# Filler matmuls on TensorE at the end of the norms, in the rank norm and in the log gates of a four-block transformer program

## The chip, the cores and the metric

The kernel runs on one core of a Trainium2 chip (trn2) as one program. The metric is the device time of one execution in microseconds (us). The median of three runs is 4041.17 us.

## The reference

Two blocks of two layers each, on 512 tokens of width 1024, all in fp32. The code below is cut to the order of the work.

```
# first block, 2 layers: mixer, norm, routed experts, norm
h = layer_norm(alpha*h + swa_sink_gqa(h, ...))      # layer 0: window attention
h = layer_norm(alpha*h + hier_moe(h, ...))          # 32 experts, 2 per token
h = layer_norm(alpha*h + mla(h, ...))               # layer 1: latent attention
      # inside mla: c = x @ w_down; cq = rms_norm(c[:384]); ckv = rms_norm(c[384:640])
h = layer_norm(alpha*h + hier_moe(h, ...))
# second block, 2 layers, on the 512 tokens and 256 context tokens
mod = silu(c) @ w_ada + b_ada                       # shifts, scales, gates
u = modulate(rmsnorm(x, g), sh1, sc1) @ w_in        # norms x0, x1
g_f = log_sigmoid(glr_f @ wg2_fw + bg_fw) / 16      # log gates lg0, lg1 (g_b likewise)
x = x + g1 * (concat(gla, short_conv, neighbourhood_attention) @ w_out)
h = modulate(rmsnorm(x, g), sh2, sc2)               # norms f0, f1
x = x + g2 * conv_ffn(h, ...)
return rmsnorm(x, final_norm_g)
```

The filler matmuls of the change compute nothing of this.

## The kernel before, in words

The program is a row of stages. Each stage is one block in which every engine has its own list of instructions, written out by hand, with semaphores between them; `end()` (L137) closes it with a barrier of all engines, in two steps of which the second follows the clearing of the semaphores. So no engine begins a stage before all have ended the one ahead. Weights are the exception: `issue` lets SyncE load the first four weight tiles of the next stage while the present one still runs.

The large products are run in fp32 split into a high and a low part (fp32r): three matmuls of up to 512 columns in place of one. ScalarE casts a weight tile (`w_high`), VectorE subtracts (`w_low`), TensorE multiplies: high by high, low by high, high by low. `fused_stream` (L694) and `stream` (L456) do this for the projections, `ffn_up` (L3331) for the feed-forward part. At the start of each of these stages TensorE waits until the first tile has gone through ScalarE and VectorE.

The change touches four places in the lists of TensorE:

- `norm` (L1061 to L1144) normalises rows on VectorE and ScalarE. TensorE has no instruction in it. It is called twice: for the two low-rank parts of the latent attention ("b_norms", the rank norm), with `issue`, and for the last norm, without. Behind the rank norm come two short stages (the rotary turn, L1155 to L1160, and a copy, L2367), and then the up projection.
- `norm_turn` (L1163 to L1371) normalises token tiles and turns them. Statistics are taken tile by tile on VectorE (L1231 to L1236), ScalarE takes the root (L1318) and normalises (L1297, L1299), TensorE transposes the tile in eight pieces of 128x128 into the eight PSUM banks (L1351), and VectorE and ScalarE empty the banks by turns with scale and shift (`evac`, L1193 and L1195). With context tokens there are two parts, tiles 0 to 3 and 4 to 5; the second part's transposes wait, bank by bank, for the first part's evacuation. Where the next stage is `fused_stream` or `ffn_up` (`"XS" in turn`), the turned rows are split here too: ScalarE casts (L1304), VectorE subtracts (L1259). With `"logits"` TensorE goes on to the router's product.
- `norm_turn` is called for the norm ahead of the latent attention (m0_ln: four tiles, with XS, and with the weighted sum of the experts' rows; VectorE ends it with L1253 and L1254), by `modulated` for the mixing norms x0 and x1 (six tiles, two parts, no XS) and the feed-forward norms f0 (six tiles, two parts, XS) and f1 (four tiles, XS). The calls with logits and the one without `turn` are left as they are.
- `log_gates` (L2732 to L2809) has TensorE transpose the low-rank columns (L2771) and multiply them by the gate weights (L2778, 12 fp32 matmuls per layer, 17 rows deep, into banks 0 to 5); VectorE and ScalarE then take log sigmoid in three rounds (L2789, L2791, L2805, L2808, L2794). The next stage is neighbourhood attention (L927, masked and reduced on VectorE at L979, with the bias tables at L2714).

The matmul at L3089, in the gated linear attention, is plain fp32 with 512 columns.

```
if "logits" in turn:
    w = turn["logits"][1]
for t in range(NTT):
    pe.wait_ge(low_v, 1 if t < NT else 2)
    pe.wait_ge(low_a, 1 if t < NT else 2)
```

These two pieces, of `norm_turn` and of `log_gates`, are the surroundings of the lines added.

Of the kernel before, what the change touches and what calls it, by code (L numbers as in the profile page):

```python
# [23 lines left out]
BANK = 512  # L24
# [96 lines left out]
class Program:  # L121
# [29 lines left out]
    def load(self, name, pairs):  # L151

        nc, sem = self.nc, self.Sems(self, name)
        loaded_sp, loaded_act = sem("loaded_sp"), sem("loaded_act")
        with nc.Block() as block:
            @block.sync
            def _(sp):
                for dst, src in pairs[0::2]:
                    sp.dma_start(dst, src).then_inc(loaded_sp, 16)
                sp.wait_ge(loaded_sp, 16 * len(pairs[0::2]))  # L160

            @block.scalar
            def _(act):
                for dst, src in pairs[1::2]:
                    act.dma_start(dst, src).then_inc(loaded_act, 16)
                if len(pairs) > 1:
                    act.wait_ge(loaded_act, 16 * len(pairs[1::2]))
        self.end(sem)

    def transpose(self, name, groups, beside=None, loads=None):  # L170

# [889 lines left out]
    def norm(self, name, tiles, kind, eps, loads=(), issue=None):  # L1061

        nc, sem = self.nc, self.Sems(self, name)
        stats, roots, scales, step, loaded = (sem(n) for n in ("stats", "roots", "scales", "step", "loaded"))
        normed, gained, biased = sem("normed"), sem("gained"), sem("biased")
        ctx = ExitStack()
        n = len(tiles)
        pieces = [[(c, min(c + 512, t[0].shape[1])) for c in range(0, t[0].shape[1], 512)] for t in tiles]  # L1070
        bn = self.sbuf(ctx, "bn", [P, n, 12])
        mv = self.sbuf(ctx, "mv", [P, n, 4])
        inv = self.sbuf(ctx, "inv", [P, n, 2])
        eps_t = self.sbuf(ctx, "eps", [P, 1])
        gains, biases = tiles[0][2] is not None, tiles[0][3] is not None
        by_act = [gains or i % 2 == 1 for i in range(n)]
        with nc.Block() as block:  # L1077
            if loads:
                @block.sync
                def _(sp):  # L1080
                    for dst, src in loads:
                        sp.dma_start(dst, src).then_inc(loaded, 16)
                    if issue:
                        issue(sp)

            @block.vector
            def _(dve):
                order = Order(dve, step)
                order.done(dve.memset(eps_t[:, :], eps))  # L1089
                for i, (src, dst, gain, bias) in enumerate(tiles):  # L1090
                    for c, (a, b) in enumerate(pieces[i]):
                        ins_ = dve.bn_stats(bn[:, i, 6 * c:6 * c + 6], src[:, a:b])  # L1092
                    order.done(ins_)
                for i in range(n):
                    ins_ = dve.bn_aggr(mv[:, i, 0:2], bn[:, i, 0:6 * len(pieces[i])])  # L1095
                order.done(ins_)
                if kind == "rms":
                    order.done(dve.tensor_tensor(mv[:, :, 2], mv[:, :, 0], mv[:, :, 0], ALU.mult))  # L1098
                    order.done(dve.tensor_tensor(mv[:, :, 2], mv[:, :, 2], mv[:, :, 1], ALU.add))  # L1099
                else:  # L1100
                    order.done(dve.tensor_copy(mv[:, :, 2], mv[:, :, 1]))
                dve.sem_inc(stats, 1)  # L1102
                dve.wait_ge(roots, 1)
                order.done(dve.reciprocal(inv[:, :, 0], mv[:, :, 3]))  # L1104
                if kind == "ln":
                    order.done(dve.scalar_tensor_tensor(out=inv[:, :, 1], in0=mv[:, :, 0], scalar=-1.0,
                                                        in1=inv[:, :, 0], op0=ALU.mult, op1=ALU.mult))
                dve.sem_inc(scales, 1)  # L1108
                if loads:
                    dve.wait_ge(loaded, 16 * len(loads))  # L1110
                for i, (src, dst, gain, bias) in enumerate(tiles):
                    if not by_act[i]:
                        dve.tensor_scalar(dst, src, inv[:, i, 0:1], None, ALU.mult)
                    if gains:
                        dve.wait_ge(normed, i + 1)  # L1115
                        dve.tensor_tensor(dst, dst, gain, ALU.mult).then_inc(gained, 1)  # L1116
                if biases:
                    dve.wait_ge(gained, n)
                    dve.tensor_tensor(dst, dst, bias, ALU.add)

            @block.scalar
            def _(act):
                act.wait_ge(stats, 1)
                act.activation(mv[:, :, 3], mv[:, :, 2], ACT.Sqrt, bias=eps_t[:, :]).then_inc(roots, 1)  # L1124
                act.wait_ge(scales, 1)
                for i, (src, dst, gain, bias) in enumerate(tiles):
                    if not by_act[i]:
                        continue
                    if kind == "rms":
                        act.activation(dst, src, ACT.Copy, scale=inv[:, i, 0:1]).then_inc(normed, 1)  # L1130
                    else:
                        act.activation(dst, src, ACT.Identity, bias=inv[:, i, 1:2],
                                       scale=inv[:, i, 0:1]).then_inc(normed, 1)

            @block.gpsimd
            def _(pool):
                if biases:
                    pool.wait_ge(loaded, 16 * len(loads))
                    for i, (src, dst, gain, bias) in enumerate(tiles[:-1]):
                        pool.wait_ge(gained, i + 1)  # L1140
                        pool.tensor_tensor(dst, dst, bias, ALU.add).then_inc(biased, 1)
                    pool.wait_ge(biased, n - 1)
        ctx.close()
        self.end(sem)  # L1144
# [18 lines left out]
    def norm_turn(self, name, tiles, kind, eps, loads=(), combine=None, finish=None, turn=None, beside=None, issue=None):  # L1163
# [19 lines left out]
        items = [(k, part) for part in range(len(turn["parts"])) for k in range(KD)] if turn else []  # L1183
# [18 lines left out]
        with nc.Block() as block:  # L1202
# [137 lines left out]
            if turn:  # L1340
                @block.tensor
                def _(pe):
                    for t in range(n):
                        part = [i for i, (a, b, _, _) in enumerate(turn["parts"]) if a <= t < b][0]
                        first = turn["parts"][part][0]
                        pe.wait_ge(normed, t + 1)
                        for k in range(KD):
                            if part and t == first:
                                i = items.index((k, part - 1))
                                pe.wait_ge(out_v if by_dve[i] else out_a, count[i])  # L1350
                            ins_ = pe.transpose(self.ps[:, k, (t - first) * P:(t - first + 1) * P],  # L1351
                                                tiles[t][1][:, k * P:(k + 1) * P], self.const("ident"))
                        ins_.then_inc(turned, 1)
                    if "logits" in turn:
                        w = turn["logits"][1]
                        m = w.shape[2]
                        pe.wait_ge(loaded, 16 * len(loads))
                        for k in range(KD):
                            pe.wait_ge(out_v if by_dve[k] else out_a, count[k])
                            for t in range(n):  # L1360
                                ins_ = pe.matmul(self.ps[:, 0, t * m:(t + 1) * m], turn["XT"][:, k, t * P:(t + 1) * P],
                                                 w[:, k, :], start=(k + t == 0), stop=(k == KD - 1),
                                                 skip_group_check=True)
                        ins_.then_inc(summed, 1)
# [1367 lines left out]
    def log_gates(self, layer, UG, LR, MX, beside, loads):  # L2732
# [8 lines left out]
        with ExitStack() as ctx:  # L2741
# [6 lines left out]
            ident = self.const("ident")  # L2748
# [7 lines left out]
            with nc.Block() as block:  # L2756
# [11 lines left out]
                def _(pe):  # L2768
# [5 lines left out]
# [3 lines that stand above are left out]
                        for d in range(2):  # L2777
                            ins_ = pe.matmul(Z(t)[:, d * QK:(d + 1) * QK], LR[:, d, t * P:(t + 1) * P],  # L2778
                                             W2[:, d * QK:(d + 1) * QK], start=True, stop=True)
                        ins_.then_inc(products, 1)  # L2780

                @block.vector
                def _(dve):
# [730 lines left out]
```

## Time and profile before

| | |
|---|---|
| runs | 4038.2, 4041.17, 4041.52 us |
| profiled execution | span 4027.6 us from the first to the last instruction, 51130 instructions; no other time of it is given. The median of the runs is 13.6 us above the span |
| TensorE (PE) busy | 3484.0 us, 87% of the span |
| VectorE (DVE) busy | 2580.3 us, 64% |
| ScalarE (ACT) busy | 2238.7 us, 56% |
| GpSimd (POOL) busy | 588.4 us, 15% |
| DMA | 643.21 MB, mean 160 GB/s |

The eight places of the change lie in the span like this (from barrier to barrier): m0_ln 818 to 858 us, rank norm 893 to 904, x0 1878 to 1899, log gates lg0 2138 to 2156, f0 2484 to 2513, x1 3090 to 3110, log gates lg1 3314 to 3332, f1 3596 to 3616.

In the profile PE is TensorE's matmuls. "PEclk" is the granted TensorE clock of a stretch as a share of full speed, and its two levels are 0.50 (1.2 GHz) and 1.00 (2.4 GHz). The row of a group of instructions gives its start, its length, the engine, the line, and in brackets how long the engine had been idle before it and what ended that.

### The profile page before, as it was taken

How to read it: one execution, taken by the hardware profiler on the slowest of the kernel's cores; microseconds unless marked ns; L12 is line 12 of the kernel's file. 1: busy time of each engine (PE TensorE's matmuls, PEld its weight loads, DVE VectorE, ACT ScalarE, POOL GpSimd, SP SyncE). 2: the span in 40 equal slices, each digit the busy share in tenths (PEclk: the TensorE clock that was granted, in tenths of full speed). 3: DMA queues.
4: the chain of work that ended last, by engine and by line, in shares of the span. 5: the costliest groups of instructions: out<-in, count | busy, mean ns of one | idle time of the engine just before them, and what ended most of it. 6: DMA issues, size and time to landing. Idle time of an engine off the chain costs nothing. (4 is left out here: it accounts for less than half of the span.)

```text
span 4027.6 us, 51130 instructions
## 1 busy us (share of the span) xinstructions
PE 3484.0 (87%) x17582; PEld 2850.1 (71%) x17582; DVE 2580.3 (64%) x3499; ACT 2238.7 (56%) x2862; POOL 588.4 (15%) x284
## 2 busy tenths in 40 slices
PE   8869999848969999857987887999997988869997
PEld 7757777647757777635887765888776877558875
DVE  4669999845569999886455555444445565645545
ACT  3549999834449999775344553333233444634433
POOL 0005333400005334400002220000000002300000
PEclk9879999979979999978998968999999998879999
DMA  3049999921049999894110000211121220012222
GB/s 108 30 155 415 418 419 415 366 97 45 26 174 419 417 417 414 343 377 198 57 50 32 2 32 33 73 62 62 55 63 45 72 64 5 1 61 102 94 86 81
DMA packets 139776, 643.21 MB, mean 160 GB/s; under 512 B 22110, under 2 KB 35808, under 8 KB 76000
## 3 DMA queue, kind: packets, MB, share of 16 engines
q1 hardware_dynamic: 129260, 623.44, 40.2%
q0 software_dynamic: 10080, 16.80, 1.1%
q8 instruction: 86, 1.41, 0.1%
q10 hardware_dynamic: 288, 1.05, 0.1%
q14 instruction: 62, 0.51, 0.0%
HBM read 636.77 MB, written 24.36 MB: 164 GB/s over the span
## 5 line engine op out<-in xcount | busy, mean ns | idle before, releaser
L1647 DVE TENSOR_TENSOR w_low<-w_raw,w_high 128x2048 fp32r<-128x2048 f32 x392 | 881.8, 2283 | 61.8 <-ACT w_high L1644 54.2
L1644 ACT CAST w_high<-w_raw 128x2048 fp32r<-128x2048 f32 x392 | 746.3, 1910 | 87.1 <-DMA w_raw<-in_moe_down_dram 39.4
L1954 PE MATMUL banks<-w_high,x_split 128*128 128x512 f32 x1024 | 421.5, 412 | 43.8 <-DVE w_low L1647 36.6
L1954 PE MATMUL banks<-w_low,x_split 128*128 128x512 f32 x1024 | 408.2, 399 | 0.0
L456 PE MATMUL banks<-w_high,x_high 128*128 128x512 f32 (+2 forms) x808 | 309.8, 383 | 53.5 <-DVE w_low L373 29.0
L337 ACT CAST w_high<-w_raw 128x512 fp32r<-128x512 f32 (+2 forms) x200 | 117.8, 589 | 421.7 <-PE banks L456 415.6
L3331 PE MATMUL banks<-x_high,w_high 128*128 128x512 f32 (+1 forms) x1056 | 318.7, 356 | 28.1 <-DVE w_low L3371 28.1
L3331 PE MATMUL banks<-x_low,w_high 128*128 128x512 f32 (+1 forms) x1056 | 318.2, 355 | 0.0
L3331 PE MATMUL banks<-x_high,w_low 128*128 128x512 f32 (+1 forms) x1056 | 317.9, 355 | 0.0
L456 PE MATMUL banks<-w_low,x_high 128*128 128x512 f32 (+2 forms) x808 | 301.9, 374 | 0.0
L456 PE MATMUL banks<-w_high,x_low 128*128 128x512 f32 (+2 forms) x808 | 301.9, 374 | 0.0
L1954 PEld LDWEIGHTS banks<-w_high,x_split 128*128 128x128 f32 x1024 | 194.4, 190 | 122.4 <-DVE w_low L1647 78.0
L1904 POOL DMA_INDIRECT expert_rows<-ys,sidx x34 | 252.4, 7425 | 125.4 <-ACT ys L2124 124.8
L3356 ACT ACTIVATE convolved<-banks,taps 128x768 f32<-128x768 f32 (+1 forms) x88 | 77.9, 885 | 297.1 <-PE banks L3331 297.1
L694 PE MATMUL banks<-w_high,x_high 128*128 128x512 f32 (+2 forms) x516 | 207.9, 403 | 30.6 <-DVE w_low L664 17.5
L371 DVE TENSOR_TENSOR x_low<-mixT,x_high 128x768 fp32r<-128x768 f32 x112 | 107.3, 958 | 187.9 <-ACT x_high L338 187.7
L1954 PEld LDWEIGHTS banks<-w_low,x_split 128*128 128x128 f32 x1024 | 195.0, 190 | 40.6
L456 PEld LDWEIGHTS banks<-w_high,x_high 128*128 128x128 f32 x808 | 155.0, 192 | 96.9 <-DVE w_low L373 43.8
L3331 PEld LDWEIGHTS banks<-x_high,w_high 128*128 128x128 f32 x1056 | 175.0, 189 | 56.9 <-issue 28.7
L3383 DVE SCALAR_TENSOR_TENSOR convolved<-banks,taps,convolved 128x511 f32<-128x511 f32 (+1 forms) x132 | 83.0, 656 | 194.1 <-ACT convolved L3356 194.1
L694 PE MATMUL banks<-w_high,x_low 128*128 128x512 f32 (+2 forms) x516 | 203.3, 394 | 0.0
L694 PE MATMUL banks<-w_low,x_high 128*128 128x512 f32 (+2 forms) x516 | 203.1, 394 | 0.0
(411 smaller groups left out, 7576.8 us busy)
## 6 DMA issues: line engine op xcount, KB each, us to landing
w_raw<-in_moe_gate_dram SPq DMA_DIRECT2D x132, 1024.0 KB, 10.5
w_raw<-in_moe_up_dram SPq DMA_DIRECT2D x132, 1024.0 KB, 10.2
w_raw<-in_moe_down_dram SPq DMA_DIRECT2D x132, 1024.0 KB, 10.9
w_raw<-in_w_ada_dram SPq DMA_DIRECT2D x48, 1024.0 KB, 12.9
w_raw<-in_ffn_w_up_dram SPq DMA_DIRECT2D x44, 1024.0 KB, 4.8
w_raw<-in_ffn_w_down_dram SPq DMA_DIRECT2D x88, 256.0 KB, 2.7
w_raw<-in_w_cols_dram SPq DMA_DIRECT2D x48, 256.0 KB, 2.6
w_raw<-in_w_out_dram SPq DMA_DIRECT2D x32, 256.0 KB, 3.0
```

The source lines that it names most:

```text
L337: act.copy(WS[0][:, rest % S, 0:w], W[:, rest, 0:w])
L371: dve.tensor_tensor(XS[1][:, rest % S, :], x_tile(k), XS[0][:, rest % S, :].bitcast(F32), ALU.subtract)
L456: ins_ = pe.matmul(psum_of(g), st[:, rest % S, a:b], mv[:, rest % S, x:y], start=start and first + second == 0, stop=stop and first == 1)
L694: ins_ = pe.matmul(psum_of(g), XS[first][:, k, t * P:(t + 1) * P], WS[second][:, u % S, 0:w], start=(i == 0 and first + second == 0), stop ...
L1644: act.copy(ex["WS"][0][:, v % HIGH, :], ex["WR"][:, v % RAW, :]).then_inc(ex["high"], 1)
L1647: dve.tensor_tensor(ex["WS"][1][:, v % LOW, :], ex["WR"][:, v % RAW, :], ex["WS"][0][:, v % HIGH, :].bitcast(F32), ALU.subtract).then_inc( ...
L1904: pool.indirect_dma_start(out=Y, out_offset=bass.IndirectOffsetOnAxis(ap=sidx[:, 0:1], axis=0), in_=YS[:, :], in_offset=None, bounds_check ...
L1954: ins_ = pe.matmul(GU[b][m], stationary(b, kk), WS[w][:, s, k * BANK:(k + 1) * BANK], start=(kk == 0 and w == 0), stop=(kk == KD - 1 and w ...
L3331: ins_ = pe.matmul(U(b, ab)[:, x:y], WS[first][:, b, at:at + P], XS[second][:, k, x:y], start=(k == 0 and first + second == 0), stop=(k == ...
L3356: act.activation(Z[:, ab, :], U(b, ab)[:, 0:ntok], ACT.Identity, bias=cv[:, bass.ds(f * 8 + (4 * ab + 3), 1)], scale=cv[:, bass.ds(f * 8 + ...
L3383: dve.scalar_tensor_tensor(out=z[:, x + 1:y], in0=u[:, x:y - 1], scalar=cv[:, bass.ds(f * 8 + 4 * ab, 1)], in1=z[:, x + 1:y], op0=ALU.mult ...
```

## The change

A new helper multiplies the identity (128x128, fp32) by the first 512 columns of the table of constants (fp32) into one whole PSUM bank, `count` times, with no semaphore; nothing reads the bank.

- in `norm` (only where `issue` is given, so in the rank norm): 10 times, into bank 0, without waiting for anything; TensorE had no work in this stage.
- in `norm_turn` without logits: behind all transposes, TensorE waits until bank 0's last part has been emptied, and then multiplies 8 times (with XS: m0_ln, f0, f1) or 3 times (x0, x1) into bank 0.
- in `log_gates`: 8 times into bank 7 right behind the products of both layers. Bank 7 held a group of transposes that ScalarE has emptied before the first product.

These are 10 + 3 x 8 + 2 x 3 + 2 x 8 = 56 matmuls in the source. Nothing is removed or moved.

```diff
+    def keep_busy(self, pe, bank, count):
+
+        for _ in range(count):
+            ins_ = pe.matmul(self.ps[:, bank, :], self.const("ident"), self.consts[:, 0:BANK], start=True, stop=True)
+        return ins_
...
@@ norm, behind the list of ScalarE
+            @block.tensor
+            def _(pe):
+                if issue:
+                    self.keep_busy(pe, 0, 10)
+
...
@@ norm_turn, behind the transposes
                         ins_.then_inc(turned, 1)
+                    if "logits" not in turn:
+                        i = items.index((0, len(turn["parts"]) - 1))
+                        pe.wait_ge(out_v if by_dve[i] else out_a, count[i])
+                        self.keep_busy(pe, 0, 8 if "XS" in turn else 3)
                     if "logits" in turn:
...
@@ log_gates, behind the products
                         ins_.then_inc(products, 1)
+                    self.keep_busy(pe, 7, 8)
```

Line numbers in the texts are those of the kernel before; in the changed kernel the matmul of `keep_busy` is L173.

## Rows read from the trace of the kernel before

**Rows 1.** Spans and mean granted clock of the core.
```profile
core 0: 4027.6 us, clock 0.918
```

**Rows 2.** Windows, TensorE: stretch, length, busy (records), PEclk, DMA share, GB/s.
```profile
859.42:864.66 5.24, 5.24 (x16) 0.50 0.50 150
864.66:869.66 5.00, 5.00 (x30) 1.00 0.21 59
1902.70:1905.72 3.02, 3.02 (x9) 0.50 0.43 128
3113.66:3117.45 3.79, 3.79 (x9) 0.50 0.42 137
2519.08:2523.53 4.45, 4.45 (x14) 0.50 0.66 236
3622.47:3626.04 3.57, 3.57 (x8) 0.50 0.67 223
```

**Rows 3.** Waits of VectorE, 3331 to 3352 us: in total, times, longest.
```profile
DVE scores L979 <- PE banks L927: 0.7, 2, 0.5
```

**Rows 4.** Timeline of L3089, then L3089 and L2778: records, ns min/median/max.
```profile
2272.09 5.38 PE L3089 MATMUL banks<-mixT,k_end 128*64 128x512 f32 x6 [2.67 <-POOL mixT L3037]
3498.26 2.79 PE L3089 MATMUL banks<-mixT,k_end 128*64 128x512 f32 x6
...
L3089 PE MATMUL banks<-mixT,k_end x144: 592/592/1117, 2272.1 to 3506.4; 128*64 128x512 f32 x144
...
L2778 PE MATMUL banks<-w_gate,lowrankT x48: 320/322/523, 2141.5 to 3323.1; 17*128 17x192 f32 x48
```

**Rows 5.** Timeline of VectorE in m0_ln.
```profile
846.93 1.53 DVE L1193 TENSOR_SCALAR qT<-banks,columns 128x512 f32<-128x512 f32 x2
...
856.00 1.22 DVE L1254 TENSOR_TENSOR H<-H,bias 128x1024 f32<-128x1024 f32 x1
```

**Rows 6.** Windows of TensorE around two idle stretches.
```profile
2039.19:2042.06 2.87, 0.00 (x0) 1.00 0.17 62
2042.41:2047.41 5.00, 2.28 (x6) 0.50 0.16 43
3941.54:3947.00 5.46, 2.61 (x11) 1.00 0.20 54
```

**Rows 7.** Timeline: VectorE in the rank norm, TensorE behind it.
```profile
902.75 0.42 DVE L1116 TENSOR_TENSOR o_rows<-o_rows,gkv 128x256 f32<-128x256 f32 x1
...
907.53 1.94 PE L685 MATMUL banks<-consts,o_rows 128*128 128x128 f32 x8 [16.00 <-PEq L139]
```

**Rows 8.** Timeline of VectorE in x0; windows of TensorE behind x0's and x1's transposes.
```profile
1896.86 1.90 DVE L1193 TENSOR_SCALAR mixT<-banks,scale,MC 128x256 f32<-128x256 f32 x4 [3.58 <-PE banks L1351]
...
1896.82:1902.70 5.88, 0.00 (x0) 0.50 0.00 0
3107.63:3110.60 2.97, 0.00 (x0) 1.00 0.00 0
```

**Rows 9.** Timeline of VectorE in f0 and f1.
```profile
2506.15 0.54 DVE L1193 TENSOR_SCALAR hiddenT<-banks,scale,MC 128x256 f32<-128x256 f32 x1 [1.71 <-PE banks L1351]
...
2510.50 1.42 DVE L1259 TENSOR_TENSOR x_low<-hiddenT,x_high 128x256 fp32r<-128x256 f32 x4
...
3612.78 2.55 DVE L1259 TENSOR_TENSOR x_low<-hiddenT,x_high 128x512 fp32r<-128x512 f32 x4
```

**Rows 10.** Windows of TensorE over f1's transposes.
```profile
3601.24:3607.39 6.15, 5.85 (x32) 0.65 0.00 1
```

**Rows 11.** Timeline: VectorE's last in the log gates, TensorE's first in attention.
```profile
2151.89 2.88 DVE L2794 SCALAR_TENSOR_TENSOR mixT<-banks,mixT 128x384 f32<-128x384 f32 x6 [3.06 <-ACT mixT L2808]
...
2155.93 0.76 PE L927 MATMUL banks<-nakT_high,naqT 128*128 128x512 f32 x1 [9.50 <-PEq L139]
...
3327.90 2.88 DVE L2794 SCALAR_TENSOR_TENSOR mixT<-banks,mixT 128x384 f32<-128x384 f32 x6 [3.06 <-ACT mixT L2808]
...
3331.94 0.77 PE L927 MATMUL banks<-nakT_high,naqT 128*128 128x512 f32 x1 [8.29 <-PEq L139]
```

## The prediction

> **What bounds the kernel now.** I read the clock first. TensorE's mean granted clock is 0.918 of full speed over a span of 4027.6 us [rows 1]. The clock has two levels, so it stood at the lower one (1.2 GHz) for 2 x (1 - 0.918) = 16% of the span, some 660 us. The change works on only eight places of it. Then I took the stretch behind each place by windows. Where TensorE has been idle at the end of a norm, the next stage's dense matmuls begin at 0.50: for 5.24 us behind the latent norm m0_ln, 3.02 and 3.79 behind the mixing norms x0 and x1, 4.45 and 3.57 behind the feed-forward norms f0 and f1 [rows 2]. The rank norm's successor I take to be like m0_ln's. Sixteen matmuls took 5.24 us there; 30 took 5.00 us right after, so sixteen would have taken 2.67 and the slow clock cost 2.6 us, 0.49 of the stretch. By that share the six stretches (20.1 us and once more 5.2) cost 12.4 us, 0.3% of the run. That is all that the norms could give back. The log gates come before attention, and there VectorE waited for TensorE's first products for only 0.7 us in the first 20 us [rows 3]: attention starts at VectorE's pace, so a warm clock gives at most that.
>
> **The price of one filler.** keep_busy multiplies plain fp32. The trace has such a matmul of 512 columns at L3089: six records in a row took 5.38 us with the clock low and 2.79 with it high. A record on its own lasts 1.12 us at the most and 0.59 at the least, so the steps are (5.38 - 1.12)/5 = 0.85 and (2.79 - 0.59)/5 = 0.44 us, of which 0.43 is taken. One fp32 matmul of the source is two records: L2778 is called 12 times per layer, 24 in all, and has 48 [rows 4]. So a filler takes **0.86 us at the high clock, 1.71 at the low**. Eight take 6.9, three 2.6, ten 8.6 at the high clock. At the low clock the rise comes after some time of dense work, 4.0 us in the mean of five stretches (5.24, 3.02, 3.79, 4.45, 3.57) [rows 2]: eight then take 4.0 + (8 - 4.0/1.71) x 0.86 = 8.9 us, three take 4.0 + 0.66 x 0.86 = 4.6. The last record ends 0.16 us later than its step.
>
> **What the fillers run beside.** Every stage ends in a barrier of all engines; I take it that TensorE reaches it only when the fillers are done. What counts is whether they end before VectorE's last instruction, and then how long TensorE still idles.
>
> - **m0_ln, 8 fillers.** VectorE empties bank 0 at 846.93 + 0.76 = 847.7 and ends at 857.22 [rows 5]. The clock is low: 847.7 + 8.9 + 0.16 = 856.8. No delay; 0.4 us of cover is left. TensorE then idles until 859.42, 2.7 us. Two idle stretches of that length lie in the trace: after 2.87 us (2039.19) the clock was low, after 2.85 us (3941.54) it stayed at 1.00 [rows 6]. Half of 2.6: **-1.3** (bounds -2.6 and 0).
> - **Rank norm, 10.** TensorE is free 16.00 us before 907.53, at 891.5; a barrier later, near 892.7, the fillers start with the clock high and end at 901.5. VectorE's last ends at 902.75 + 0.42 = 903.17 [rows 7]. No delay. But two short stages follow, and TensorE idles until 907.5, for 6.0 us, twice what lowered the clock at 2039: **0** (bounds -2.6 and 0).
> - **x0 and x1, 3 each.** VectorE empties bank 0's last part first of four in 1.90 us from 1896.86, so the fillers start at 1897.4 with 1.4 us of cover until 1898.76. At the high clock (2.6 + 0.16) they end 1.3 us late, at the low one (4.6 + 0.16) 3.4 late. The same code left the clock low in x0 and high in x1 [rows 8], so I take the mean: 2 x 2.35 = **+4.7** (bounds +2.6 and +6.8). After that, TensorE idles as long as it takes the next stage to cast and subtract its first operands, from 1898.76 to 1902.70 = 3.9 us; that is over 2.9, so nothing comes back.
> - **f0, 8.** From 2506.15 + 0.54 = 2506.7; VectorE ends at 2511.92 [rows 9]. Low clock: 2515.8, 3.8 us late; high clock: 2513.8, 1.8 late. It was low, with transposes coming one by one: **+3.3**. From VectorE's end to the first matmul at 2519.08 are 7.2 us, which stay idle: no gain.
> - **f1, 8.** The transposes end at 3607.39 with the clock high [rows 10]; bank 0 takes 0.77 us, as in m0_ln (two in 1.53) [rows 5]. From 3608.2 to 3615.2; VectorE ends at 3615.33 [rows 9]. **+0.2**, for 0.1 us of cover (+1.9 if low). Then 7.2 us idle, no gain.
> - **Log gates, 8 each.** TensorE is free 9.50 us before 2155.93 and 8.3 before 3331.94, at 2146.4 and 3323.6; clock low. Fillers end at 2155.5 and 3332.7. VectorE ends at 2154.77 and 3330.78 [rows 11]: **+0.7 and +1.9** (clock never rising: +5.6 and +6.8). Only the barrier's one us is idle then, so attention starts warm: 2 x **-0.3**, at most -0.7 each.
>
> The sum is -1.3 + 0 + 4.7 + 3.3 + 0.2 + 0.7 + 1.9 - 0.6 = **+8.9 us**. The profiled span of 4027.6 us has no total of its own; the runs' median of 4041.17 lies 13.6 above it, launch and end, which the change leaves alone. Forecast: 4050.1 us. The terms' own bounds, not all at once, give +4 to +14. What a measurement can tell from no change is 0.2%, 8.1 us, and the forecast lies just over it.
>
> **Transposes and the clock.** From 3601.24 to 3607.39 TensorE did nothing in f1 but transposes by the identity (L1351), 32 of them, and the clock of that stretch is 0.65 in the mean [rows 10]: it came in at 0.50, and for 0.3 of the time, the last 1.8 us, it was at full speed. Transposes lifted the clock here. The Trainium skill (TensorE: Matmul & The Clock Gate, Part 4) says the opposite, that the full clock does not engage for transposes. The trace disagrees. By the page, fillers behind transposes would always start at the low clock, which is the fourth rival below.
>
> **Rivals.**
> 1. *The barrier does not hold the others back* (TensorE passes it with fillers still in flight, so casts of the next stage run under them). Then the delays go, except 0.7 us in lg1 where the matmuls themselves queue; x0 starts warm (fillers end 1902.1, matmuls 1902.70: -1.5), x1 idles some 2.8 us and gains half of 1.9, m0_ln -1.3, attention -0.6. Sum -3.6: 4037.6. It decides wherever fillers outlast VectorE, five places of eight. For it: no row shows a stage that TensorE ended last. Against: every stage begins on all engines at once. Chance 0.10. **This is the case that ends on the other side**, not slower.
> 2. *The clock survives all the idle ends.* Then 12.4 + 0.6 come back against delays of 10.8: -2.2, 4039.0. Against it are rows 6 and the idle of 6 to 7 us. 0.05; with rival 1 as well (-12.4 - 0.6 + 0.7, 4029) 0.02.
> 3. *A filler is one record, not two.* Eight take 5.4 us from low, three 2.6. x0 is 1.4 late, x1 0, f0 0.4, the rest covered; TensorE idles longer after it and nothing comes back: +1.8, 4043. Against it is 48 for 24. 0.06.
> 4. *Fillers always start low* (the page's rule, if f1's rise was luck). x0 and x1 3.4 each, f0 3.8, f1 1.9: the sum becomes +13.2, 4054. 0.07.
> 5. *Constants never lift the clock.* Eight take 13.7 us and 0.27 for the last record: m0_ln +4.4, x0 and x1 +4.0 each, f0 +8.7, f1 +6.8, the gates +5.6 and +6.8: +40, 4081 and more. The rise under L1351, whose one operand is the identity too, speaks against it. 0.03.
>
> **How the numbers follow.** The forecast has 0.67. By its bounds three fifths of it lie above 8.1 us: 0.40, and with rivals 4 and 5, slower is 0.50. Same is 0.27 from it and 0.18 from rivals 1, 2 and 3, 0.45. Faster is rivals 1 and 2 together and the edge of 1: 0.05. The range of 8 in 10 goes from 4039 (rivals 2 and 3 in, 1 out) to 4057 (rival 4 in, 5 out).
>
> **What will show it.** 112 new records of L173 between 0.59 and 1.12 us. The barriers behind x0, x1, f0 and the gates later by 1 to 4 us, behind m0_ln and the rank norm not. The first matmuls behind x0, x1, f0, f1 and the rank norm still at 0.50; attention's at 1.00. I am wrong if ACT's first cast after x0 starts before the last filler ends, if one of the six stretches of rows 2 is warm more than now and then, or if the records are 56.

## The result, and the profile after

The changed kernel takes 4051.11 us in the median of 8 runs (4044.0 to 4061.2), the kernel before 4041.35 us beside it (8 runs, 4031.7 to 4044.5). The ratio is 1.0033, 95% interval 1.0023 to 1.0043: 13.3 us slower, between 9.3 and 17.4. One execution of all in this document (of e7, below) took 11,408 us at a mean granted clock of 0.442; every ratio leaves it out.

The profiled execution of the change took 4049.33 us with a span of 4047.5 us, 19.9 more than the span in [rows 1]. Its core and its clock:

```profile
core 0: 4047.5 us, clock 0.925
```

The granted clock rose (0.918 to 0.925) and the time rose with it. The page has TensorE busy for 62 us more (3484.0 us before):

```profile
PE 3546.0 (88%) x17694; PEld 2867.4 (71%) x17694; DVE 2579.0 (64%) x3499; ACT 2238.5 (55%) x2862; POOL 583.8 (14%) x284
```

The new line of the source, L173: durations in ns (min/median/max), first and last start.

```profile
L173 PE MATMUL banks<-consts x112: 592/592/1223, 847.5 to 3634.5; 128*128 128x512 f32 x112
```

So 56 matmuls are 112 records. The eight stretches of fillers, by windows of TensorE (stretch, length, busy (records), PEclk, DMA share, GB/s), in the order m0_ln, rank norm, x0, x1, f0, f1, lg0, lg1:

```profile
847.46:856.01 8.55, 8.54 (x16) 0.83 0.00 0
891.59:900.43 8.84, 8.82 (x20) 1.00 0.57 158
1894.81:1899.35 4.54, 4.52 (x6) 0.62 0.00 0
3121.73:3127.20 5.47, 5.45 (x6) 0.52 0.00 0
2509.71:2518.29 8.58, 8.56 (x16) 0.83 0.00 0
3627.98:3635.13 7.15, 7.13 (x16) 1.00 0.00 1
2151.38:2159.92 8.54, 8.53 (x17) 0.83 0.01 5
3340.88:3350.30 9.42, 9.41 (x17) 0.76 0.13 51
```

(x17 in the gates: the last gate product lies in the window too.) VectorE's last instruction in m0_ln, x0, x1, f0, f1, lg0 and lg1, by the timeline; these answer to [rows 5, 8, 9, 11]:

```profile
855.65 1.22 DVE L1265 TENSOR_TENSOR H<-H,bias 128x1024 f32<-128x1024 f32 x1
...
1894.22 1.90 DVE L1204 TENSOR_SCALAR mixT<-banks,scale,MC 128x256 f32<-128x256 f32 x4 [3.58 <-PE banks L1362]
...
3121.14 1.90 DVE L1204 TENSOR_SCALAR mixT<-banks,scale,MC 128x256 f32<-128x256 f32 x4 [2.98 <-PE banks L1362]
...
2513.48 1.42 DVE L1270 TENSOR_TENSOR x_low<-hiddenT,x_high 128x256 fp32r<-128x256 f32 x4
...
3632.47 2.55 DVE L1270 TENSOR_TENSOR x_low<-hiddenT,x_high 128x512 fp32r<-128x512 f32 x4
...
2155.80 2.88 DVE L2810 SCALAR_TENSOR_TENSOR mixT<-banks,mixT 128x384 f32<-128x384 f32 x6 [3.07 <-ACT mixT L2824]
...
3346.17 2.88 DVE L2810 SCALAR_TENSOR_TENSOR mixT<-banks,mixT 128x384 f32<-128x384 f32 x6 [3.06 <-ACT mixT L2824]
```

The fillers end 3.2 us behind VectorE in x0 (1899.35 against 1896.12), 4.2 in x1, 3.4 in f0, 1.2 in each of the gates, 0.1 in f1; in m0_ln and the rank norm they end before it. Where they end late, the next stage starts late: after x0 ScalarE's first cast comes 0.9 us behind the last filler.

```profile
1900.25 0.62 ACT L343 CAST w_high<-w_raw 128x512 fp32r<-128x512 f32 x1 [4.10 <-ACTq L337]
```

What came back, by windows over the first matmuls of the next stage; these answer to [rows 2]. In order: behind m0_ln (two windows), x0, x1, f0, f1, and the start of attention behind lg0 and lg1:

```profile
859.07:860.58 1.51, 1.51 (x8) 1.00 0.27 63
860.58:863.99 3.41, 3.41 (x12) 0.50 0.64 203
1903.25:1908.47 5.22, 5.22 (x15) 0.50 0.32 104
3131.24:3137.27 6.03, 6.03 (x14) 0.50 0.27 87
2525.43:2529.70 4.27, 4.27 (x13) 0.50 0.76 242
3642.29:3645.86 3.57, 3.57 (x8) 0.50 0.65 232
2160.83:2166.83 6.00, 3.49 (x16) 1.00 0.01 3
3351.21:3355.73 4.52, 2.59 (x12) 1.00 0.00 0
```

Attention alone starts at the full clock and keeps it over these windows; it falls there too, 7.2 us (lg0) and 4.6 us (lg1) behind the barrier. Behind m0_ln the clock holds for 1.5 us and falls while TensorE is multiplying. Behind x1 the slow stretch is now longer than before, 6.03 us against 3.79 [rows 2]. Behind x0 it is 5.22 us against 3.02 [rows 2], but that is no effect of the fillers: the kernel before has 4.78 and 5.72 us there in two further traces (e9, then e1, below).

```profile
1902.91:1907.69 4.78, 4.78 (x14) 0.50 0.37 110
...
1902.01:1907.73 5.72, 5.72 (x18) 0.50 0.28 92
```

From barrier to barrier, in us, with three more traces that the experiments brought: e1 and e9 are the kernel before, word for word, and e10 is the change, word for word.

| stage | before | e1 | e9 | change | e10 | predicted |
|---|---|---|---|---|---|---|
| m0_ln | 39.95 | 39.96 | 39.91 | 40.00 | 40.26 | 0 |
| behind it (down projection) | 34.48 | 34.35 | 33.98 | 33.66 | 33.64 | -1.3 |
| rank norm | 11.15 | 11.15 | 11.16 | 11.16 | 11.17 | 0 |
| up projection | 58.49 | 58.40 | 58.21 | 55.52 | 58.31 | 0 |
| x0 | 21.22 | 21.18 | 21.22 | 24.40 | 24.48 | +2.35 |
| u0 (projection behind x0) | 238.67 | 240.97 | 240.01 | 242.15 | 242.16 | 0 |
| lg0 | 17.66 | 17.80 | 17.39 | 18.54 | 18.61 | +0.7 |
| attention 0 | 94.71 | 94.69 | 94.82 | 94.20 | 94.80 | -0.3 |
| f0 | 28.36 | 28.35 | 28.36 | 31.72 | 31.87 | +3.3 |
| ffn_up0 (behind f0) | 380.74 | 380.77 | 387.76 | 387.66 | 387.65 | 0 |
| x1 | 20.39 | 20.39 | 20.72 | 24.88 | 24.88 | +2.35 |
| u1 (behind x1) | 203.62 | 203.72 | 203.65 | 204.84 | 205.07 | 0 |
| lg1 | 17.76 | 17.91 | 17.68 | 18.22 | 18.62 | +1.9 |
| attention 1 | 80.58 | 80.42 | 80.38 | 79.52 | 79.50 | -0.3 |
| f1 | 20.10 | 20.09 | 20.10 | 20.22 | 20.17 | +0.2 |
| span | 4027.6 | 4033.9 | 4040.6 | 4047.5 | 4057.7 | |

The puzzle in the first pair of traces was ffn_up0: 6.92 us longer, more than any stage with a filler in it (4.5 at the most), and not at its start but evenly over the whole stage, at the full clock.

### The profile page after: what moved, and what is told of

The parts are those of the page before. It is cut to its first block and busy times, and to the rows that moved or that the text cites. A ratio compares the mean times of both kernels' runs of the same rounds, so it can differ in the third digit from the quotient of the medians.

```text
span 4047.5 us, 51354 instructions
## 1 busy us (share of the span) xinstructions
PE 3546.0 (88%) x17694; PEld 2867.4 (71%) x17694; DVE 2579.0 (64%) x3499; ACT 2238.5 (55%) x2862; POOL 583.8 (14%) x284
```

## The experiments

**e1: the kernel before, word for word**, as a measure of what two traces of one kernel differ by.

> The kernel before, once more, for a second trace of it. The two traces at hand differ by 19.9 us of span but the medians of eight runs by only 9.8. In the first trace the feed-forward up stage of layer 0 took 380.7 us, in the trace of the changed kernel 387.7, at the same granted clock, with matmul steps 1.9% longer from the first to the last. Theory A (the fillers cost what they push the barriers, about 12 us, and the slower pace is chance that a kernel without fillers shows too): the median is within 0.15% of before, and over repeated traces that stage takes now 381, now 388 us. Rival B (the fillers cause the slower pace): it takes 380.7 us here again and whenever there are no fillers.

Measured: 4038.25 us, ratio 1.0006 (0.9996 to 1.0016). Its stages differ from those of before by up to 2.3 us (u0), with nothing changed.

**e2: only the fillers that VectorE's work covers** (m0_ln, rank norm, f1).

```diff
-                    if "logits" not in turn:
+                    if "XS" in turn and len(turn["parts"]) == 1 and "logits" not in turn:
...
-                    self.keep_busy(pe, 7, 8)
```

> Fillers only where they end before VectorE does: m0_ln (8), rank norm (10), f1 (8). Theory A: no barrier moves; the stage behind m0_ln is shorter by 0 to 2.6 us, the one behind the rank norm by 0 to 3, the one behind f1 by nothing: 0 to -5 us in all, 4036 to 4041, the same or a little faster than before. Rival B: as slow as the change as a whole (+8 to +10), since fillers anywhere do it.

Measured: 4036.47 us, ratio 1.0004 (0.9995 to 1.0014). The stages m0_ln, rank norm and f1 took 40.03, 11.15 and 20.25 us, the down projection 33.65. Covered fillers cost nothing and bring 0.6 us (33.65 against the mean of 34.27 in the three traces of the kernel before).

**e3: only the uncovered ones** (x0, x1, f0, log gates).

```diff
-                if issue:
-                    self.keep_busy(pe, 0, 10)
+                pass
...
-                    if "logits" not in turn:
+                    if not ("XS" in turn and len(turn["parts"]) == 1) and "logits" not in turn:
```

> Fillers only where they outlast VectorE: x0 and x1 (3 each), f0 (8), the log gates (8 each). Theory A: all of the loss is here. Barriers later by 1.3 to 4.5 us in x0 and x1 each, 1.8 to 3.9 in f0, 0.4 to 1.9 in each of the log gates; 0.5 to 1 us back in each attention: +7 to +14 us in all, 4048 to 4055, more than the whole change. Rival B: the same loss as with any fillers, +8 to +10.

Measured: 4047.58 us, ratio 1.0035 (1.0019 to 1.0050), the whole loss of the change. x0 22.79, f0 31.94, x1 24.87 us; x0 lost less than in the change because its fillers met the full clock earlier (2.8 us for the three), and in lg0 (17.08 us) the eight ended 0.4 us before VectorE did.

**e4: twice the fillers in x0, x1 (6) and f0 (16)**, the rest as in the change.

```diff
-                        self.keep_busy(pe, 0, 8 if "XS" in turn else 3)
+                        self.keep_busy(pe, 0, 6 if "XS" not in turn else 16 if len(turn["parts"]) > 1 else 8)
```

> The whole change, but twice the fillers in x0, x1 (6 each) and f0 (16). Theory A (the barrier waits for each of them, at 0.86 us once the clock is high): each of x0 and x1 longer by another 2.6 to 3.5 us, f0 by another 6.9, in sum 12 to 14 us more than the change, about 4064. Rival C (the barrier does not wait for TensorE's fillers): the same as the change, 4051.

Measured: 4063.55 us, ratio 1.0062 (1.0046 to 1.0079). f0 took 38.60 us, 6.88 more than in the change for 8 fillers: 0.86 each. x0 took 27.08 and x1 27.44, 2.7 and 2.6 more for three. The log gates, whose eight fillers are those of the change, took 20.46 and 20.41 us in this trace, against 18.54 and 18.22: the clock rose later there, and the fillers ended 2.8 and 2.2 us behind VectorE, where it had been 1.2. The barrier waits for every filler at the price of two records, and the rivals "the barrier doesn't hold the others back" and "one record" fall. The 32 records of f0:

```profile
2518.77:2534.22 15.45, 15.45 (x32) 0.90 0.00 1
```

After these four, ffn_up0 had taken 380.8 (before, e1, e2), 380.6 (e4) and 387.7 us (the change, e3). The numbers of fillers ahead of it are 0, 0, 18, 48 and 37, 19. It looked as if the place of ffn_up0's loop in TensorE's list of instructions, which every filler ahead of it moves ("place" below), or what f0's eight leave behind ("f0"), set the pace.

**e5: one filler in all, in x0. e6: the change with nine in f0.**

```diff
@@ e5
-                    if "logits" not in turn:
+                    if name == "x0":
...
-                        self.keep_busy(pe, 0, 8 if "XS" in turn else 3)
+                        self.keep_busy(pe, 0, 1)
@@ e6
-                        self.keep_busy(pe, 0, 8 if "XS" in turn else 3)
+                        self.keep_busy(pe, 0, 3 if "XS" not in turn else 9 if len(turn["parts"]) > 1 else 8)
```

> One filler in all, in x0 behind its last eviction; nothing else of the change (the rank norm and the layer norm keep an empty TensorE block, which adds one branch ahead of the FFN). The question is why the matmuls of ffn_up0 take 0.1767 us a step instead of 0.1734 in the change and in e3 but not in e2 and e4. Theory 'place': it is where the loop's instructions lie in TensorE's instruction stream, which every filler (4 instructions: two weight loads and two matmuls) and every branch ahead of it moves. Counted so, the loop is moved by 150 in the change and 77 in e3 (slow; 6 and 5 modulo 8), by 74 in e2, 194 in e4 and 0 in before (normal; 2, 2 and 0 modulo 8). Here it is moved by 5: ffn_up0 takes 387.7 us, 7 more than before, and the kernel 4041.35 + 0.9 + 7 - about +8 us, ratio 1.002. Theory 'f0': it is what f0's eight fillers leave behind (the clock's phase, a bank): none here, so ffn_up0 takes 380.7 and the kernel is at 1.0002.

> The change with 9 fillers in f0 instead of 8, all else the same. Theory 'place': ffn_up0's loop is moved by 154 instructions (2 modulo 8, as e2 and e4): ffn_up0 takes 380.7 us, f0 0.86 us more than in the change, and the span is about 6 us under that of the change (4047.5), near 4041.5; ratio 1.0018. Theory 'f0': what eight fillers in f0 leave, nine leave too: ffn_up0 387.7 us, span 4048.4, ratio 1.0035.

Measured: e5 4042.05 us, ratio 1.0004 (0.9994 to 1.0014), ffn_up0 387.75. e6 4050.57 us, ratio 1.0033 (1.0017 to 1.0048), ffn_up0 380.34. Both traces did what "place" said, but both medians did not: e5 without a loss, e6 with the change's whole loss though its trace has the fast pace. So the profiled traces alone can't answer it: a pace that belongs to the kernel would have moved the medians.

**e9, e10, e11: the kernel before, the change and e5 again, word for word.**

> The kernel before, word for word, profiled a third time. The stretch ffn_up0 took 380.74 us in its first trace and 380.77 in e1's; 387.7 in the change, e3, e5, e7 (385.6 with its head at full clock) and e8. Theory 'place' (where the loop lies in TensorE's instructions decides its pace): 380.7 again. Theory 'chance' (the pace is drawn anew in each execution, whatever the kernel: e6's median stands at 1.0033 though its profile has the fast pace, e5's at 1.0004 though its profile has the slow one, and the unchanged kernel alone spans 4031 to 4048 us): 380.7 or 387.7, about as often.

> The change, word for word, profiled again. Theory 'place': ffn_up0 387.7 us as in its first trace. Theory 'chance': 380.7 or 387.7; with 380.7 the span is near 4040.5.

> e5 (one filler in x0) profiled again. Theory 'place': 387.7 us for ffn_up0, as in e5. Theory 'chance': either; over these three runs and e1 'chance' leaves about 1 in 8 that all repeat their first value.

Measured: ffn_up0 took 387.76 us in the unchanged kernel (380.74 and 380.77 in its other traces) and 380.81 in e5's kernel (387.75 in its other). "Place" is refuted. TensorE over the same 250 us of the unchanged kernel, before and then e9:

```profile
2600.00:2850.00 250.00, 250.00 (x1444) 1.00 0.18 66
```

```profile
2600.00:2850.00 250.00, 250.00 (x1417) 1.00 0.18 63
```

And of e5 and then e11, one filler both:

```profile
2600.00:2850.00 250.00, 250.00 (x1417) 1.00 0.18 63
```

```profile
2600.00:2850.00 250.00, 250.00 (x1444) 1.00 0.17 63
```

Same clock, 1.9% fewer matmuls, with nothing changed in the kernel. Of the 14 traces six have the fast pace (before, e1, e2, e4, e6, e11) and eight the slow one. So 7 of the 19.9 us between the first two spans are no effect of the change.

**e8 and e7: can fillers win?** e8 keeps to what fits under VectorE (m0_ln 8, rank norm 11, gates 6, f0 3, f1 8, x0 and x1 none). e7 adds one in the rope behind the rank norm, and fillers past the barrier, at the head of the stage where TensorE waits for its first weights.

```diff
@@ e8 and e7
-                    self.keep_busy(pe, 0, 10)
+                    self.keep_busy(pe, 0, 11)
...
-                    if "logits" not in turn:
+                    if "XS" in turn and "logits" not in turn:
...
-                        self.keep_busy(pe, 0, 8 if "XS" in turn else 3)
+                        self.keep_busy(pe, 0, 3 if len(turn["parts"]) > 1 else 8)
...
-                    self.keep_busy(pe, 7, 8)
+                    self.keep_busy(pe, 7, 6)
@@ e7 alone: rope_halves, stream, ffn_up
+            @block.tensor
+            def _(pe):
+                self.keep_busy(pe, 0, 1)
...
+                if name[0] == "u":
+                    self.keep_busy(pe, 0, 3)
                 tiles(pe, tile)
...
                     pe.sem_inc(multiplied, 4)
+                    self.keep_busy(pe, 0, 6)
```

> As e7 without the fillers in the rope and at the heads of u and of the FFN: 8 in the layer norm, 11 in the rank norm, 6 in the log gates, 3 in f0, 8 in f1. Theory A: no barrier later by more than 0.3 us; gains only b_up -0.4 to -3, na0 -0.5, na1 -1; ratio 0.9990 to 0.9997. ffn_up0 (moved by 114 instructions, 2 modulo 8) at 380.7. What e7 has over this one is the worth of the heads. Rival (a filler at a tail delays the barrier even where VectorE is later): f0 and the log gates +0.5 each, ratio 1.000.

> Fillers only where they can't hold a barrier back, and in the idle heads of the next stages too: 8 in the layer norm, 11 in the rank norm and 1 in the rope that follows, 6 in the log gates, 3 at the end of f0, 8 in f1, none in x0 and x1; and behind the barrier, ahead of the first weights, 3 at the start of u0 and u1 (3.2 us of idle TensorE) and 6 at the start of the two FFN halves (6.3 us). Theory A (a filler costs 0.86 us only where the barrier waits for it, and keeps the clock high for the work behind): no barrier later, the first matmuls of u and of the FFN at full clock; b_up -3, na0 and na1 -0.5 and -1, u0 and u1 -1 each, ffn_up0 and ffn_up1 -1.5 each: span -6 to -9, ratio 0.998. The loop of ffn_up0 is moved by 156 (4 modulo 8, not seen yet): 380.7 or 387.7. Rival (the low stretches only move to another place in the same stage): b_up -0.4 to -3, the rest zero, ratio 0.9995 to 1.0005.

Measured: e8 4039.22 us, ratio 1.0002 (0.9992 to 1.0011); f0 28.36 us, where the three ended 0.8 us before VectorE, and x0, without fillers, 21.23: neither barrier moved. In lg1 the six ended 0.2 us behind VectorE. e7 4031.39 us, ratio 0.9989 (0.9978 to 0.9999), beside the same runs of the kernel before. TensorE in e7: from f0's fillers to those of the head, the first matmuls of ffn_up0, the same two for f1 and ffn_up1, then the heads of u0 and u1:

```profile
2506.93:2518.63 11.70, 9.82 (x18) 0.86 0.03 8
2519.14:2523.60 4.46, 4.46 (x25) 1.00 0.67 231
3614.35:3627.98 13.63, 12.52 (x28) 1.00 0.03 7
3628.55:3632.95 4.40, 4.40 (x19) 1.00 0.63 238
1898.02:1903.10 5.08, 5.08 (x7) 0.55 0.15 46
3115.40:3120.86 5.46, 5.46 (x7) 0.50 0.16 48
```

And the first matmuls of ffn_up0 and ffn_up1 in e8:

```profile
2521.75:2526.15 4.40, 4.40 (x13) 0.50 0.70 242
...
3634.37:3638.89 4.52, 4.52 (x11) 0.50 0.63 232
```

With the idle head filled, both halves of the FFN begin at the full clock: 25 matmuls in 4.46 us where e8 has 13 in 4.40. ffn_up0 took 385.61 us against 387.78 in e8 (both at the slow pace), ffn_up1 250.46 against 252.68: 2.2 us each, where 1.5 was expected (without head fillers ffn_up1 takes 252.2 to 253.4 us in the twelve other traces, so its part is 1.7 to 2.9). At the heads of u the fillers met the low clock, took 5.1 and 5.5 us instead of 2.6 and made the first real matmul 1.4 us late.

**e12: e7 without the three at the heads of u.**

```diff
-                if name[0] == "u":
-                    self.keep_busy(pe, 0, 3)
```

> e7 without the three fillers at the heads of u0 and u1, which started at the low clock there (5.1 and 5.5 us instead of 2.6) and made the first matmul of u 1.37 us late (4.58 us behind the barrier instead of 3.21). Kept: 8 in the layer norm, 11 in the rank norm, 1 in the rope, 6 in the log gates, 3 + 6 around the barrier of ffn_up0, 8 + 6 around that of ffn_up1. Theory A: u's first matmul at 3.21 again and up to 1.4 us less in each of u0 and u1, the FFN halves begin at full clock as in e7 (2.2 us less each than in e8); ratio 0.998 to 0.999, at or below e7's 0.9989. Rival (e7's gain was in u): ratio back at e8's 1.0002.

Measured: 4036.05 us, ratio 0.9994 (0.9985 to 1.0003). ffn_up1 is again at 250.55 us, but ffn_up0 took 386.53: in this trace the clock was low for the first 3.4 us of the head, and its fillers outlasted the idle time (first matmul 6.8 us behind the barrier, not 6.2). u1 took 204.65, more than e7's 204.23, with no filler in x1 or at its own head: its first matmul came 3.2 us behind the barrier as it should, but the clock stayed low for the first 5.35 us of matmuls.

```profile
3125.83:3131.18 5.35, 5.35 (x13) 0.50 0.31 98
```

The 1.4 us expected did not show; e7 and e12 can't be told apart. The heads are worth about 0.1% at best, and e7's interval reaches up to 0.9999.

## Why the prediction was right, and where not

The forecast was +8.9 us, 4050.1; the medians differ by 9.8 and the ratio says +13.3. The likeliest case came true, rather on its upper side: +8.9 lies just under the lower end of 9.3 to 17.4. The mechanism held, fillers that outlast VectorE push the barrier. The terms were less good than their sum: x0 and x1 came 2.9 us over theirs and u1, put at nothing, 1.3, while lg1 stayed 1.3 below its term. That these partly cancel is luck.

- **Price of a filler**: 0.86 us at the high clock, two records. Shown by e4 (6.88 us for eight) and by the count of 112. The low price, 1.71 us, shows in x1: 5.45 us for three. The longest record is 1.22 us, not 1.12.
- **The barrier waits for TensorE**: shown by e4 and by the table.
- **f0, f1, rank norm, m0_ln**: +3.4 for +3.3, +0.1 for +0.2, 0 for 0. The down projection came 0.6 us down where 1.3 was taken. I had halved between a stretch all fast and one all slow, and neither came: in all eight traces with fillers in m0_ln the first matmul met the high clock, and 0.1 to 1.5 us later it fell, under the matmuls. The gates gave +1.0 and +0.6 for +0.7 and +1.9, attention -0.2 and -0.9 for -0.3 each (means of two traces against three); the second is beyond the bound of 0.7 that I took from VectorE's waits. Attention 1 took 79.49 to 79.67 us in the eight traces with fillers in lg1 and 80.05 to 80.58 in the six without, so this gain stands clear of the spread. The lg1 term was too high: its fillers took 9.42 us, near the 9.1 foreseen, but they started 8.2 us ahead of VectorE's end (3340.88 and 3349.05), not 7.2, so they were 1.2 us late. The +1.0 and +0.6 themselves are not firm: lg0 took 16.88 to 17.80 us and lg1 17.68 to 18.68 in the traces without fillers there.
- **x0 and x1, the mis-sized term.** I took the mean of a low and a high clock, 2.35 us each. They came 3.2 and 4.4 late, 7.6 instead of 4.7, beyond the upper bound of 6.8. The low case itself was too short: I let the clock rise after 4.0 us of fillers, 4.6 us for three. In x1 the clock fell 0.9 us before the last transpose ended and rose only 0.2 us before the last of the six records did (5.45 us). In all four traces with three fillers in x1 (the change, e3, e6, e10) x1 took 24.87 or 24.88 us. What I read as a toss-up came out alike each time there.
- **"Nothing comes back" behind x0 and x1 was too kind to x1.** u1 took 204.84 to 205.07 us in those four traces and 203.60 to 203.86 in seven of the eight without fillers at x1 or u1's head. The slow stretch at its start grew from 3.79 to 6.03 us: the clock fell 2.4 us behind x1's barrier and rose at 9.2, where before it fell at 0.2 and rose at 7.0. As I read the traces, u1's length follows the moment of that rise, and fillers only shift it. Two traces say so. The eighth without fillers there, e12, rose at 8.6 us and took 204.65. e4, with six fillers in x1, rose at 6.7 us and took 203.54. So three fillers in x1 cost 1.3 us in u1 each time here, but a filler isn't needed for such a loss. For u0 nothing is shown: the change has 242.15, e2 without a filler there 242.09, and e3, with three in x0, 238.32.
- **The sum**: by stages, -0.6 + 3.2 + 2.3 + 1.0 - 0.2 + 3.4 + 4.4 + 1.3 + 0.6 - 0.9 + 0.1 = 14.6 us, and 12.3 without u0. The ratio's +13.3 lies between. The up projection (-1.5 in these means) is left out of it; with it the sum is 13.1. Its 55.52 us in the first trace look like luck: e10 has 58.31. In the other traces a second slow stretch of 3.4 us comes some 18 us into it; only the change's first trace and e7 (57.04) lack it, two of the eight with fillers in the rank norm and none of the six without. That the fillers have a part in it is not shown.
- **The base**: I put 13.6 us of launch and end between span and median. The change's profiled execution lies 1.8 us above its span (4049.33 and 4047.5), e9's too (4042.35 and 4040.6). No run shows 13.6 us of launch and end. If the gap was 1.8 us in the trace of before too, that execution took about 4029.4 us and was simply a quick one, the fast pace of ffn_up0 among its reasons. The forecast stood, since only the difference was added to a median.
- **Transposes and the clock.** In f1 of the change the clock rose under the transposes again, and their last 1.7 us ran at full speed:

```profile
3620.95:3627.09 6.14, 5.83 (x32) 0.64 0.01 1
3625.37:3627.09 1.72, 1.71 (x16) 1.00 0.00 0
```

  By the rule of the Trainium skill (TensorE: Matmul & The Clock Gate, Part 4) the fillers of f1 would have started low; they ran at 1.00 from the first. The trace disagrees with it, as before. (The Trainium skill speaks there of TensorE's transpose mode. The kernel calls `pe.transpose`, and its 32 transposes are 32 records, where a plain fp32 matmul is two; the trace doesn't name the mode.)

## What to carry to other kernels

A filler is free only while another engine's work still outlasts it: ahead of a barrier, each one beyond that costs its full length, for the barrier holds every engine. How many fit isn't fixed: the same eight in lg0 ended between 0.4 us before and 2.8 us behind VectorE, by when the clock rose. To warm the clock for a stage (worth 0.1% at best here), put the filler where the idle time that lowers it lies, here behind the barrier while the first weights are cast, and check that it also runs at the high clock, for at the low one it takes twice as long and delays what it should help. Before explaining a difference of one stage between two traces, profile the unchanged kernel again: three traces of it differed by 13 us.

## What the runs showed of the hardware

- One stage of one kernel has two paces at the same granted clock: ffn_up0 in 380.8 or 387.8 us (1444 or 1417 matmuls in 250 us), which of them changes from one execution to the next. The slow pace has a pattern. In the median step from a matmul of 512 columns to the next, five of the six fast traces have 230 ns for each of the three products (e6: 231 to 232). All eight slow traces have 232, 236 and 241 ns, one for each product, and which product has which changes from trace to trace. ffn_up1 showed no such split (252.2 to 253.4 us without head fillers). What draws it is open.
- The clock fell while TensorE was busy: behind m0_ln it dropped 1.5 us into back-to-back matmuls, and in x1 under the last transposes. In x1, filling part of the idle stretch moved the fall into the next stage's matmuls rather than removing it.
